# Order of rounding, mask building and copies on VectorE and ScalarE in a two-part transformer kernel: eight small moves between queues

## The chip, the core and the metric

The kernel runs on one core of a Trainium2 chip, batch 1, 256 rows of 1024 features (S = 256, D = 1024). The metric is device time in microseconds (us) of one execution. TensorE (PE) multiplies; VectorE (DVE), ScalarE (ACT) and GpSimd (POOL) do the rest; SyncE (SP) only issues the loads of weights.

## The reference, cut to what matters

```
for i in range(2):                       # first_block
    h = rms_norm(x, norm_mix[i])
    x = x + (dsa_moba_mixer(h, ...) if i == 0 else nsa_mixer(h, ...))
    x = x + memory_cross_attention(rms_norm(x, norm_mem[i]), rms_norm(mem, ...), ...)
    x = x + swiglu(rms_norm(x, norm_ffn[i]), ffn_w_in[i], ffn_w_out[i])
for l in range(2):                       # second_block
    proj = _rmsnorm(x, g_mix[l]) @ w_in[l]
    ...                                  # convolution, neighbourhood, dilated and window attention
    mixed = jnp.sum(gates * branch, axis=2)
    x = x + mixed @ w_out[l]
    x = x + _conv_ffn(_rmsnorm(x, g_ffn[l]), w_up[l], ffn_conv_w[l], ffn_conv_b[l], w_down[l])
```

`rms_norm` divides each row by the root of its mean square. The dilated attention needs a mask that also holds the logarithm of how often a key is counted. Everything is float32.

## The kernel before, in words

Eight blocks of code run one after the other: `block_dsa_moba` (names that begin with ab), `block_memory_ffn` (mf), `block_nsa` (nsa), `block_memory_ffn` again, and then twice `block_branches` (mix) and `block_conv_ffn` (cffn). Each block writes out a queue for each engine by hand; an engine works through its own queue in order, and semaphores are the only ties between queues. The order of the code lines in each queue is therefore the schedule.

**Weights.** Every matrix product is done in three products of rounded parts. A chunk of weights (1 MB, 128x2048) arrives in one of 4 raw slots. ScalarE rounds it (`w.round_to`, L143, writes w_hi), VectorE takes the rest (`w.cut_to`, L144, writes w_lo), and TensorE waits for w_lo. There are 3 slots for the pairs, so rounding chunk c also waits until TensorE has used chunk c - 3. The first four chunks of a block are loaded in the block before, and the first of them is already rounded and cut there. A `stationary_job` is one chunk used as the stationary operand: 48 matmuls of 256 columns. Features are rounded (L297) and cut (L303) in the same way.

**Row factors.** The product is taken before the norm is known. The sums of squares (`rows.square`, L290, ScalarE) go to GpSimd (`rows.factors`, L312 to L318), VectorE spreads the factor (`row_factors.dve`, L332), TensorE turns it (`row_factors.pe`, L338), and ScalarE stores it (`row_factors.act`, L343). In mix and cffn TensorE did this between job 0 and job 1.

**Attention.** `Attention` runs a pipeline over pairs of heads. In step i TensorE makes scores i (L740), turns the exponentials of i - 1 (L750), multiplies with the values of i - 2 (L765) and then does one piece of other work. VectorE masks and takes the maximum (L795), and copies the turned exponentials from PSUM (L810); ScalarE takes the exponential (L778). Scores i wait for the masking of i - 1. In ab VectorE also finds the largest 64 index scores between the steps (`top_rounds`, L1341, L1342), and the other work of TensorE is a third of a memory projection (L882 to L884). In mix it is a whole gate job of 48 matmuls. GpSimd sums the convolution's taps during those steps (L2519).

**Masks.** `make_masks` in mix builds the dilated mask on VectorE in the pauses of the projection: its last piece (j == 2, L2658 to L2668, five operations) stands ahead of the fourth projection's copy (L484). The mask is first used at step 4.

**Tail of mix.** Eight times TensorE forms the four branch products of one tile (L2855 to L2857), VectorE multiplies by the gates (L2771), GpSimd adds (L2528, L2530), ScalarE rounds (L2616) and VectorE cuts (L2758). Cuts of the next chunks stand after every second tile. TensorE may begin tile j only when L2771 of tile j - 2 is done.

## Time and profile before

| | |
|---|---|
| Median of 3 runs | 1686.68 us (1684.48, 1686.98, 1686.68) |
| The profiled execution's own time | 1684.49 us |
| Its span, first to last instruction | 1682.7 us |
| PE busy | 1626.0 us (97%) |
| DVE, ACT, POOL busy | 1096.4, 885.1, 456.2 us |
| Mean granted TensorE clock | 0.995 |

Busy PE time includes the overlap of matmuls in flight, so the pauses between starts of matmuls say more than the share. Line numbers in this part are those of the kernel before.

### The profile page before, as it was taken

Reading aid. Unit: us, or ns where it says so; the run is one execution under the profiler, and the core shown is the slowest. Engines: PE = TensorE matmul, PEld = TensorE weight load, DVE = VectorE, ACT = ScalarE, POOL = GpSimd, SP = SyncE. Lnnn points to the kernel's source line nnn. Section 1 sums busy time; section 2 is a strip of 40 time slices with the busy share of each in tenths; the row PEclk is TensorE's granted clock in tenths of the full one; section 3 lists DMA queues with packets and bytes.
Section 4 is the critical chain, followed back from the end, with each engine's and each line's share of the span. In section 5 each row is a group of like instructions: output and inputs, shape, how many; then the busy total and the mean of one; then the engine's idle time right before and its main releaser. Section 6 shows DMA issues by size and latency. Waiting matters only on the chain. (4 is left out here: it accounts for less than half of the span.)

```text
span 1682.7 us, 26946 instructions
## 1 busy us (share of the span) xinstructions
PE 1626.0 (97%) x10929; PEld 1465.7 (87%) x10929; DVE 1096.4 (65%) x1546; ACT 885.1 (53%) x1385; POOL 456.2 (27%) x476
## 2 busy tenths in 40 slices
PE   8989899999999999999999999999999999999999
PEld 7857799987887879998888998999888899889997
DVE  6875656545576765655577668677646866867773
ACT  7454554434455555443446746566445674665652
POOL 2500200002341120000237805144213790504430
PEclk9999999999999999999999999999999999999999
DMA  7522466556340236665554434766556444376652
GB/s 275 171 75 91 110 181 195 178 199 207 103 150 26 76 101 169 187 193 185 177 191 151 151 126 131 197 182 192 180 160 211 155 150 129 127 197 178 189 187 75
DMA packets 287068, 265.30 MB, mean 158 GB/s; under 512 B 12257, under 2 KB 247521, under 8 KB 286945
## 3 DMA queue, kind: packets, MB, share of 16 engines
q1 hardware_dynamic: 286944, 263.59, 50.4%
q8 instruction: 86, 1.41, 0.4%
q14 instruction: 38, 0.30, 0.1%
HBM read 262.52 MB, written 1.05 MB: 157 GB/s over the span
## 5 line engine op out<-in xcount | busy, mean ns | idle before, releaser
L144 DVE TENSOR_TENSOR w_lo<-w_raw,w_hi 128x2048 fp32r<-128x2048 f32 (+2 forms) x244 | 568.8, 2334 | 296.7 <-ACT w_hi L143 294.5
L1863 PE MATMUL bank<-h_hi,w_hi 128*128 128x256 f32 x1984 | 566.2, 285 | 11.9 <-issue 4.6
L143 ACT ACTIVATE w_hi<-w_raw 128x2048 fp32r<-128x2048 f32 (+2 forms) x244 | 462.4, 1901 | 207.4 <-PE bank L529 117.4
L1864 PE MATMUL bank<-h_lo,w_hi 128*128 128x256 f32 x1984 | 561.9, 283 | 0.0
L1865 PE MATMUL bank<-h_hi,w_lo 128*128 128x256 f32 x1984 | 561.9, 283 | 0.0
L1863 PEld LDWEIGHTS bank<-h_hi,w_hi 128*128 128x128 f32 x1984 | 380.8, 192 | 16.4 <-issue 10.9
L1864 PEld LDWEIGHTS bank<-h_lo,w_hi 128*128 128x128 f32 x1984 | 381.0, 192 | 0.1
L1865 PEld LDWEIGHTS bank<-h_hi,w_lo 128*128 128x128 f32 x1984 | 380.9, 192 | 0.0
L456 PE MATMUL bank<-w_hi,h_hi 128*128 128x512 f32 (+1 forms) x288 | 113.5, 394 | 5.4 <-DVE w_lo L144 3.4
L2925 POOL TENSOR_TENSOR cffn_hidden<-cffn_conv 128x256 f32<-128x256 f32 x44 | 72.2, 1642 | 164.3 <-ACT cffn_conv L2955 164.3
L457 PE MATMUL bank<-w_lo,h_hi 128*128 128x512 f32 (+1 forms) x288 | 111.9, 389 | 0.0
L458 PE MATMUL bank<-w_hi,h_lo 128*128 128x512 f32 (+1 forms) x288 | 111.9, 388 | 0.0
L2519 POOL TENSOR_TENSOR mix_conv<-mix_conv,mix_gates 128x512 f32<-128x512 f32 x60 | 106.2, 1769 | 20.9 <-ACT mix_gates L2556 12.6
L1760 ACT ACTIVATE mf_gate<-mf_gate 128x256 f32<-128x256 f32 x44 | 18.4, 418 | 129.8 <-DVE mf_gate L1809 129.8
L2989 DVE SCALAR_TENSOR_TENSOR cffn_conv<-cffn_before,cffn_cols,cffn_conv 128x255 f32<-128x255 f32 x176 | 75.0, 488 | 0.0
L456 PEld LDWEIGHTS bank<-w_hi,h_hi 128*128 128x128 f32 x288 | 54.3, 189 | 18.8 <-DVE w_lo L144 4.3
L2470 POOL MEMSET mix_padded<- 128x572 f32 x2 | 1.1, 575 | 240.4 <-POOLq L1718 187.2
L458 PEld LDWEIGHTS bank<-w_hi,h_lo 128*128 128x128 f32 x288 | 54.2, 188 | 10.9
L2977 DVE TENSOR_TENSOR cffn_before<-bank,cffn_row_factors 128x512 f32<-128x512 f32 x44 | 30.4, 691 | 50.4 <-PE bank L1865 50.4
L457 PEld LDWEIGHTS bank<-w_lo,h_hi 128*128 128x128 f32 x288 | 54.3, 188 | 10.1
L2556 ACT ACTIVATE mix_gates<-mix_padded,mix_cols 128x256 f32<-128x256 f32 x120 | 50.8, 496 | 14.7 <-POOL mix_conv L2519 14.7
L2528 POOL TENSOR_TENSOR mix_feat<-mix_feat 128x512 f32<-128x512 f32 x16 | 37.7, 2353 | 71.9 <-DVE mix_feat L2771 71.9
(444 smaller groups left out, 2884.0 us busy)
## 6 DMA issues: line engine op xcount, KB each, us to landing
w_raw<-in_w_in SPq DMA_DIRECT2D x48, 1024.0 KB, 5.0
w_raw<-in_ffn_w_in SPq DMA_DIRECT2D x88, 512.0 KB, 5.1
w_raw<-in_w_up SPq DMA_DIRECT2D x88, 512.0 KB, 5.2
w_raw<-in_ffn_w_out SPq DMA_DIRECT2D x22, 1024.0 KB, 4.9
w_raw<-in_w_down SPq DMA_DIRECT2D x22, 1024.0 KB, 4.9
w_raw<-in_nsa_w_in SPq DMA_DIRECT2D x10, 1024.0 KB, 5.1
w_raw<-in_mem_w_kv SPq DMA_DIRECT2D x8, 1024.0 KB, 5.1
w_raw<-in_w_branch SPq DMA_DIRECT2D x8, 1024.0 KB, 5.1
```

What stands on the lines that cost most here:

```text
L143: return act.activation(hi, raw, ACT.Copy)
L144: return dve.tensor_tensor(self.lo[:, cut_slot, 0:k * n], raw, hi.bitcast(F32), ALU.subtract)
L456: pe.matmul(bank, x_hi, whi[:, k, :], start=(f == 0), stop=False)
L457: pe.matmul(bank, x_hi, wlo[:, k, :], start=False, stop=False)
L458: ins = pe.matmul(bank, x_lo, whi[:, k, :], start=False, stop=(f == KD - 1))
L1863: pe.matmul(out, h, hi[:, f, :], start=(f == 0), stop=False)
L1864: pe.matmul(out, h, lo[:, f, :], start=False, stop=False)
L1865: ins = pe.matmul(out, l, hi[:, f, :], start=False, stop=(f == KD - 1))
L2519: pool.tensor_tensor(conv[:, :, :], conv[:, :, :], taps[tap % 4], ALU.add).then_inc(cv_sum, 1)
L2556: act.activation(taps[tap % 4][:, n, :], u, ACT.Copy, scale=weight).then_inc(cv_tap, 1)
L2925: pool.tensor_tensor(hidden[:, j % 2, :], conv[:, j % 2, 0, :], conv[:, j % 2, 1, :], ALU.mult)\
L2989: dve.scalar_tensor_tensor(out=dst, in0=src, scalar=tap(2 * side, tile), in1=dst, op0=ALU.mult, op1=ALU.add).then_inc(sides, 1)
```

## The change

Eight edits to the queues; no arithmetic is added or taken away.

1. In mix and cffn, ScalarE rounds chunk 1 before the squares and chunk 2 behind them, and VectorE cuts chunk 1 before it spreads the factor. TensorE turns the factor in the middle of job 1 instead of between jobs 0 and 1.
2. In ab, the copies of turned exponentials go from VectorE to ScalarE (`copier="act"`), where the copy of pair i - 1 stands behind the exponentials of pair i.
3. In ab, ScalarE rounds the memory chunk before the second memory copy (`act_next(1)` ahead of `act(1)`).
4. In ab, VectorE waits for the turning of the last keys on GpSimd (`hn.wait_done(dve, 5)`) before it cuts the next memory chunk.
5. In ab, the cut of the memory chunk after that goes from before the attention to its step 1.
6. In mix, the five mask operations go to the attention's steps 0 to 3, behind each step's cut.
7. In the tail of mix, one more chunk is cut before tile 0 and none after tile 1.
8. In mf, the first maximum over the scores stands ahead of the second sum of squares.

```diff
@@ Attention.act
+            if i and self.copier == "act":
+                self.copy_turned(act, i - 1)
             if between is not None:
                 between(act, i)
+        if self.copier == "act":
+            self.copy_turned(act, len(self.pairs) - 1)
+
+    def copy_turned(self, e, j):
+        e.wait_ge(self.turned, j + 1)
+        if j >= 2:
+            e.wait_ge(self.out, j - 1)
+        dims = [[S, 2], [1, self.pairs[j]["keys"]]]
+        to, of = free(self.k.turned[:, j % 2, :], dims), free(self.k.bank[6 + j % 2][:, :], dims)
+        if self.copier == "act":
+            e.activation(to, of, ACT.Copy).then_inc(self.copied, 1)
+        else:
+            e.tensor_copy(to, of).then_inc(self.copied, 1)
@@ block_dsa_moba
-        att = Attention(k, "att", pairs, lambda i, u: (4 + u, i % 2 * S))
+        att = Attention(k, "att", pairs, lambda i, u: (4 + u, i % 2 * S), copier="act")
...
                 mem.act(act, 0)
+                mem.act_next(act, 1)
                 mem.act(act, 1)
-                mem.act_next(act, 1)
                 turn.act(act)
...
+                hn.wait_done(dve, 5)
                 mem.dve(dve, 0)
                 dve.wait_ge(const, 2)
-                mem.dve(dve, 1)
                 turn.dve(dve)
...
+                    if i == 1:
+                        mem.dve(dve, 1)
@@ block_memory_ffn
+                att.dve_peaks(dve, 0)
                 att.dve_mean(dve, 1)
-                att.dve_peaks(dve, 0)
@@ stationary_job
+        if tile == 0 and middle is not None:
+            middle(pe)
@@ block_branches, and alike in block_conv_ffn
                 rows.round(act, range(4, KD))
+                w.round_to(act, 1)
                 for t in range(T):
                     rows.square(act, t, 1)
-                w.round_to(act, 1)
+                w.round_to(act, 2)
                 row_factors.act(act)
...
                 rows.cut(dve, range(4, KD))
+                w.cut_to(dve, 1)
                 row_factors.dve(dve)
-                w.cut_to(dve, 1)
...
-                    stationary_job(k, pe, conv_chunks[i], k.bank[6 + i], rows, None, i == 0)
-                    if i == 0:
-                        row_factors.pe(pe)
+                    stationary_job(k, pe, conv_chunks[i], k.bank[6 + i], rows, None, i == 0, row_factors.pe if i else None)
@@ block_branches, masks and tail
+                def behind(dve, i):
+                    cut(dve, AHEAD + i)
+                    make_counts(dve, i)
+
+                att.dve(dve, finish, step, behind)
...
-                w.cut_to(dve, mix_chunks[0] + 1)
+                w.cut_to(dve, mix_chunks[0] + 2)
...
-                    if j % 2 == 1:
+                    if j >= 3 and j % 2 == 1:
                         w.cut_to(dve, mix_chunks[0] + j // 2 + 2)
```

`make_counts` holds the five operations of the old j == 2 piece: two in step 0 and one each in steps 1, 2 and 3.

VectorE's queue at the start of cffn, before (cffn_spread is the spread row factor):

```order
L303 SCALAR_TENSOR_TENSOR h_lo<-bank,ffn_gain,h_hi 128x256 x4
L332 COPY cffn_spread<-row_stat 128x256
L144 TENSOR_TENSOR w_lo<-w_raw,w_hi 128x2048 x2
L2977 TENSOR_TENSOR cffn_before<-bank,cffn_row_factors 128x512
L144 TENSOR_TENSOR w_lo<-w_raw,w_hi 128x2048
```

The same place of the changed kernel (L2977 is now L2999):

```order
L303 SCALAR_TENSOR_TENSOR h_lo<-bank,ffn_gain,h_hi 128x256 x4
L144 TENSOR_TENSOR w_lo<-w_raw,w_hi 128x2048
L332 COPY cffn_spread<-row_stat 128x256
L144 TENSOR_TENSOR w_lo<-w_raw,w_hi 128x2048
L2999 TENSOR_TENSOR cffn_before<-bank,cffn_row_factors 128x512
```

One cut went ahead of the spread; the other stayed between the spread and the first scaled product.

ScalarE's queue in ab from the memory copies (mem_kv) into the attention, before (ab_att is the buffer of the exponentials):

```order
L901 ACTIVATE mem_kv<-bank,ab_mem_stat 128x512 x2
L143 ACTIVATE w_hi<-w_raw 128x2048
L404 ACTIVATE ab_feat<-bank 128x512 x6
L404 ACTIVATE ab_feat<-bank 128x256
L778 ACT_TABLE_LOAD
L778 ACTIVATE ab_att,ab_att_stat<-ab_att,ab_att_stat 128x128 x8
L778 ACTIVATE ab_att,ab_att_stat<-ab_att,ab_att_stat 128x256 x8
```

The same place of the changed kernel, up to the fourth pair (L901 is now L909, and L797 is the copy):

```order
L909 ACTIVATE mem_kv<-bank,ab_mem_stat 128x512
L143 ACTIVATE w_hi<-w_raw 128x2048
L909 ACTIVATE mem_kv<-bank,ab_mem_stat 128x512
L404 ACTIVATE ab_feat<-bank 128x512 x6
L404 ACTIVATE ab_feat<-bank 128x256
L778 ACT_TABLE_LOAD
L778 ACTIVATE ab_att,ab_att_stat<-ab_att,ab_att_stat 128x128 x4
L797 ACTIVATE ab_att<-bank 128x2x128
L778 ACTIVATE ab_att,ab_att_stat<-ab_att,ab_att_stat 128x128 x2
L797 ACTIVATE ab_att<-bank 128x2x128
L778 ACTIVATE ab_att,ab_att_stat<-ab_att,ab_att_stat 128x128 x2
```

The rounding went between the two memory copies, and a copy stands behind each pair's exponentials from the second pair on.

VectorE's queue in mix around the masks, before (mix_centred and mix_sig serve as scratch):

```order
L661 TENSOR_TENSOR mix_proj<-mix_proj,mix_vectors 128x2x256
L2658 TENSOR_SCALAR mix_centred<-mix_dil 128x512
L2660 TENSOR_SCALAR mix_sig<-mix_dil 128x512
L2663 TENSOR_TENSOR mix_centred<-mix_centred,mix_sig 128x512
L2665 TENSOR_SCALAR mix_sig<-mix_dil 128x512
L2668 TENSOR_TENSOR mix_dil<-mix_centred,mix_sig 128x512
L484 TENSOR_SCALAR mix_proj<-bank,row_stat 128x512
```

In the changed kernel they stand in the attention; of its steps 1 and 2 (L811 masks, L2725 is a gate's product, L799 the copy):

```order
L144 TENSOR_TENSOR w_lo<-w_raw,w_hi 128x2048
L2674 TENSOR_SCALAR mix_centred<-mix_dil 128x512
L2675 TENSOR_SCALAR mix_sig<-mix_dil 128x512
L811 ISA mix_att,mix_att_stat<-bank,mix_bias 128x256
L811 ISA mix_att_stat 128x1
L811 ISA mix_att,mix_att_stat<-bank,mix_bias 128x256
L811 ISA mix_att_stat 128x1
L2725 TENSOR_TENSOR mix_gates<-bank,mix_row_factors 128x512
L799 COPY mix_att<-bank 128x512
L144 TENSOR_TENSOR w_lo<-w_raw,w_hi 128x2048
L2679 TENSOR_TENSOR mix_centred<-mix_centred,mix_sig 128x512
```

The fourth projection's copy now follows the head norm at once, and the masking of steps 1 to 4 has mask work ahead of it.

## Rows read from the trace of the kernel before

**Rows 1.** The page: span, and busy time of the engines.

```profile
span 1682.7 us, 26946 instructions
PE 1626.0 (97%) x10929; PEld 1465.7 (87%) x10929; DVE 1096.4 (65%) x1546; ACT 885.1 (53%) x1385; POOL 456.2 (27%) x476
```

**Rows 2.** What PE waited for: us in total, times, longest us.

```profile
PE bank L1863 <- issue: 4.6, 4, 2.1
PE bank L2855 <- DVE mix_feat L2771: 4.1, 4, 1.3
PE bank L1527 <- ACT mf_att L1600: 3.9, 2, 2.0
PE bank L1863 <- DVE w_lo L144: 3.8, 4, 1.2
PE bank L765 <- DVE ab_att L810: 3.8, 4, 1.4
```

**Rows 3.** Timeline, start of the first mix block: start, duration, instruction, idle before.

```profile
827.69 1.57 ACT L297 ACTIVATE h_hi<-bank,mix_gain 128x256 fp32r<-128x256 f32 x4 [2.97 <-PEq L1718]
...
832.91 2.27 DVE L144 TENSOR_TENSOR w_lo<-w_raw,w_hi 128x2048 fp32r<-128x2048 f32 x1
...
833.62 0.38 PE L338 MATMUL bank<-ident,mix_att 128*128 128x128 f32 x2
835.23 0.39 PE L1863 MATMUL bank<-h_hi,w_hi 128*128 128x256 f32 x1 [1.23 <-DVE w_lo L144]
```

**Rows 4.** Timeline of PE, start of the second cffn block.

```profile
1497.45 0.38 PE L338 MATMUL bank<-ident,cffn_spread 128*128 128x128 f32 x2
1498.51 0.39 PE L1863 MATMUL bank<-h_hi,w_hi 128*128 128x256 f32 x1 [0.68 <-DVE w_lo L144]
```

**Rows 5.** Timeline, end of the memory projection in ab.

```profile
84.93 1.91 ACT L143 ACTIVATE w_hi<-w_raw 128x2048 fp32r<-128x2048 f32 x1
86.73 3.29 ACT L404 ACTIVATE ab_feat<-bank 128x512 f32<-128x512 f32 x7
...
90.08 0.49 PE L740 MATMUL bank<-ab_feat 64*128 64x128 f32 x4 [1.30 <-ACT ab_feat L404]
```

**Rows 6.** Timeline, attention steps 4, 9 and 11 in ab.

```profile
97.22 0.70 PE L740 MATMUL bank<-ab_feat 64*128 64x256 f32 x4
...
115.32 2.29 DVE L144 TENSOR_TENSOR w_lo<-w_raw,w_hi 128x2048 fp32r<-128x2048 f32 x1
...
119.90 0.80 PE L740 MATMUL bank<-ab_feat 64*128 64x128 f32 x4
```

**Rows 7.** Stretch; length, busy PE, PEld, DVE, ACT, POOL (x), PEclk, DMA share, GB/s.

```profile
118.60:125.40 6.80, 6.80 (x26) 4.43 (x25) 4.84 (x20) 1.62 (x9) 0.00 (x0) 0.50 0.47 154
```

**Rows 8.** Timeline, end of the projection in the first mix block.

```profile
884.83 0.69 ACT L470 ACTIVATE mix_proj<-bank,row_stat 128x512 f32<-128x512 f32 x1 [4.46 <-PE bank L458]
...
887.21 0.74 DVE L484 TENSOR_SCALAR mix_proj<-bank,row_stat 128x512 f32<-128x512 f32 x1
...
888.11 1.65 POOL L674 TENSOR_TENSOR mix_hn_stat<-mix_hn_stat,half_power 128x8 f32<-128x8 f32 x1
...
891.59 2.30 DVE L144 TENSOR_TENSOR w_lo<-w_raw,w_hi 128x2048 fp32r<-128x2048 f32 x1
```

**Rows 9.** Timeline of POOL, convolution sums of the first mix block.

```profile
899.22 4.12 POOL L2519 TENSOR_TENSOR mix_conv<-mix_conv,mix_gates 128x512 f32<-128x512 f32 x3
909.63 25.45 POOL L2519 TENSOR_TENSOR mix_conv<-mix_conv,mix_gates 128x512 f32<-128x512 f32 x13 [6.29 <-ACT mix_gates L2556]
```

**Rows 10.** Timeline, tail of the first mix block.

```profile
1012.04 1.91 ACT L143 ACTIVATE w_hi<-w_raw 128x2048 fp32r<-128x2048 f32 x1
...
1018.75 2.28 DVE L144 TENSOR_TENSOR w_lo<-w_raw,w_hi 128x2048 fp32r<-128x2048 f32 x1
...
1024.27 1.29 DVE L2771 TENSOR_TENSOR mix_feat<-bank,mix_gates 128x512 f32<-128x512 f32 x2
```

**Rows 11.** Timeline of DVE, memory attention of the first mf block.

```profile
180.16 0.69 DVE L1637 TENSOR_REDUCE mf_q_stat<-mf_q_squared 128x4 f32<-128x512 f32 x1 [1.69 <-ACT mf_q_squared L1579]
```

More of the change, by code:

```diff
@@ L701, with __init__ @@
 class Attention:
-    def __init__(self, k, name, pairs, place=None):
+    def __init__(self, k, name, pairs, place=None, copier="dve"):
         s = k.sems
-        self.k, self.pairs = k, pairs
+        self.k, self.pairs, self.copier = k, pairs, copier
         self.place = place or (lambda i, u: (4 + i % 2, u * S))
@@ L801, in dve @@
                 between(dve, i)
-            if 1 <= i <= n:
-                j = i - 1
-                p = self.pairs[j]
-                dve.wait_ge(self.turned, j + 1)
-                if j >= 2:
-                    dve.wait_ge(self.out, j - 1)
-                w = p["keys"]
-                dims = [[S, 2], [1, w]]
-                dve.tensor_copy(free(self.k.turned[:, j % 2, :], dims), free(self.k.bank[6 + j % 2][:, :], dims))\
-                    .then_inc(self.copied, 1)
+            if 1 <= i <= n and self.copier == "dve":
+                self.copy_turned(dve, i - 1)
             if i >= 3 and self.pairs[i - 3]["last"]:
@@ L1847, in block_memory_ffn, with stationary_job @@
         k.close()
-def stationary_job(k, pe, c, bank, features, free_bank, first=False):
+def stationary_job(k, pe, c, bank, features, free_bank, first=False, middle=None):
     w, hi, lo = k.weights, features.hi, features.lo
@@ L2654, in make_masks, with make_counts @@
                                     .then_inc(mask_step, 1)
-                    if j == 2:
-                        count, value = centred[:, :, :], sig[:, :, :]
+                def make_counts(dve, i):
+                    count, value = centred[:, :, :], sig[:, :, :]
+                    if i == 0:
                         dve.wait_ge(mask_step, 7)
                         dve.tensor_scalar(count, dil[:, :, :], 0.0, NEG, ALU.is_equal, ALU.mult).then_inc(mask_step, 1)
-                        dve.wait_ge(cv_mul, 2)
                         dve.tensor_scalar(value, dil[:, :, :], 2.0, 8 * math.log(2.0), ALU.is_equal, ALU.mult)\
                             .then_inc(mask_step, 1)
+                    if i == 1:
                         dve.wait_ge(mask_step, 9)
                         dve.tensor_tensor(count, count, value, ALU.add).then_inc(mask_step, 1)
+                    if i == 2:
                         dve.wait_ge(mask_step, 10)
@@ L2666, in make_masks @@
                             .then_inc(mask_step, 1)
+                    if i == 3:
                         dve.wait_ge(mask_step, 11)
                         dve.tensor_tensor(dil[:, :, :], count, value, ALU.add).then_inc(mask_step, 1)
+                        dve.wait_ge(mask_step, 12)
                 def bias_table(dve):
@@ L2690, in sums @@
                         w.cut_to(dve, project.last[j] + 3)
-                    if j < 3:
+                    if j < 2:
                         make_masks(dve, j)
@@ L2745, in _ @@
                 dve.wait_ge(biased, 1)
-                dve.wait_ge(mask_step, 12)
-                att.dve(dve, finish, step, lambda dve, i: cut(dve, AHEAD + i))
+                def behind(dve, i):
+                    cut(dve, AHEAD + i)
+                    make_counts(dve, i)
+                att.dve(dve, finish, step, behind)
                 dve.wait_ge(ln_act, 3)
@@ L2935, in _ @@
                 rows.round(act, range(4, KD))
+                w.round_to(act, 1)
                 for t in range(T):
                     rows.square(act, t, 1)
-                w.round_to(act, 1)
+                w.round_to(act, 2)
                 row_factors.act(act)
@@ L2965, in _ @@
                 rows.cut(dve, range(4, KD))
+                w.cut_to(dve, 1)
                 row_factors.dve(dve)
-                w.cut_to(dve, 1)
                 dve.wait_ge(cols_in, 16)
@@ L2999, in _ @@
                 for j in range(KF):
-                    stationary_job(k, pe, up[j], k.bank[j % 4], rows, (scaled, j - 3) if j >= 4 else None, j == 0)
-                    if j == 0:
-                        row_factors.pe(pe)
+                    stationary_job(k, pe, up[j], k.bank[j % 4], rows, (scaled, j - 3) if j >= 4 else None, j == 0,
+                                   row_factors.pe if j == 1 else None)
                 down.pe(pe, lambda pe, f: pe.wait_ge(hid_lo, f + 1))
```

## The prediction, made before the changed kernel ran

> **What bounds the kernel.** I read the page first. TensorE is busy for 1626.0 us of a span of 1682.7 [rows 1], so at most 56.7 us of visible pauses can be won, whatever the other engines do. The next view is the list of what TensorE waited for; a handful of waits carry most of it, and the change touches five of them [rows 2]: 3.8 us in four waits of a stationary job for a cut (w_lo), 4.6 us in four waits put down to "issue", 3.8 us in four waits of the value products for VectorE's copies in ab, 4.1 us in four waits in the tail of mix, 3.9 us in two waits for the first exponentials in mf. Together that is 20.2 us. The timeline around each then tells what ended last, and what would end last next. The profiled execution took 1684.49 us, 1.8 more than its span; the other two runs took about 2.3 us more than it.
>
> **Term 1, row factors.** In the first mix block TensorE turned the factors from 833.62, which takes 0.23 us, and job 1 began at 835.23 [rows 3]: 1.38 us lost to the cut of chunk 1, which began at 832.91 because the squares and the factor stood ahead. Now ScalarE starts rounding when the features are done at 829.26 [rows 3] and takes 1.9 us [rows 5], and VectorE cuts from 831.15 to 833.4 (2.27). That is just in time for job 0's end at 833.62. The squares slip by 1.9 us and the factor is spread at about 834.1; TensorE wants it in the middle of job 1, which is 24 matmuls or 2.9 us behind 833.6, so at 836.5. That leaves 2.4 us. Chunk 2 is cut by about 837.5 (two rounds of 1.9 and a cut), and wanted when job 1 ends at 839.6. So the stall goes and I see none in its place. In cffn the same arithmetic gives 1498.51 - 1497.45 - 0.23 = 0.83 [rows 4], and the cut of chunk 1 is over at about 1497.3 against a job that ends at 1497.45. Two mix and two cffn blocks: 2 x 1.38 + 2 x 0.83 = **4.4 us**. Lower bound 2.5, if the cut of chunk 1 comes half a microsecond late four times; upper 4.4.
>
> **Term 2, attention in ab.** First the moved rounding: ScalarE rounded at 84.93 for 1.9 us and only then copied the seven turned groups, and the first scores waited for the last copy until 90.08 [rows 5]. The rounding now fits into the wait between the two memory copies, so the copies start near 84.9 and end near 88.2: 1.8 us won. The new wait of VectorE for GpSimd costs nothing: nothing else is queued behind it but a cut that TensorE wants near 88.7, and it lets GpSimd finish before that cut. The cut moved into step 1 does cost. It is 2.29 us [rows 6] ahead of the masking of step 2, VectorE has some 0.9 us of slack there, and scores 3 wait for that masking: 1.4 us lost. So step 4 begins only 0.4 us sooner than 97.22 [rows 6].
>
> From there VectorE does not copy any more, and the four waits for its copies, 3.8 us [rows 2], go. In their place: behind the exponentials of step 7 ScalarE now has a copy (0.6), the memory copy (0.6) and a rounding (1.9), 3.1 us ahead of the exponentials of step 8, of which TensorE's step hides 2.0; 1.1 us lost. In step 9 the cut of 2.29 us still delays the masking of step 10, 0.5 us lost. Sum: 1.8 - 1.4 + 3.8 - 1.1 - 0.5 = **2.6 us**.
>
> The clock comes on top. TensorE was granted half its clock (1.2 instead of 2.4 GHz) from 118.6 to 125.4 [rows 7], directly behind two of these waits, and was busy throughout: at full clock the same work takes 3.4 us less, or 2.9 if the waits that would show again are taken off. With the waits gone I expect the fall not to come, **2.9 us**; the bounds are 0 and 3.4. Step 11 would then begin near 115.8 instead of 119.90 [rows 6].
>
> **Term 3, masks.** VectorE's copy of the fourth projection began at 887.21 though ScalarE's began at 884.83 [rows 8]: the five mask operations were in between, 2.4 us. What follows, however, waits for GpSimd as well: its power for the third head norm ended at 889.76 [rows 8], and only then comes the norm and the cut of the second gate chunk at 891.59, for which TensorE waited (two of the waits called "issue", up to 2.1 us [rows 2]). If GpSimd gains nothing, the head norm starts 0.4 us sooner; if GpSimd runs unhindered while VectorE is idle, it ends near 889.0 and the cut starts 1.3 us sooner. I take 1.2: the mask operations ran beside GpSimd's, and they are the only work there that leaves. Two blocks: **2.4 us**, between 0.8 and 4.2.
>
> In the attention of mix the same 2.8 us of VectorE lie in four steps of 7 us or more, each with some 3 us of idle VectorE. The masking of a step comes 0.4 to 1.0 us later, the copy too, and TensorE wants that copy at the earliest 2 us after it is ready now. Cost zero while that cover holds; if it is gone, each step costs what is above it.
>
> Here a rule speaks against the change. A sum of GpSimd takes 4.12/3 = 1.37 us while VectorE is quiet and 25.45/13 = 1.96 us in the attention [rows 9], so the two do hinder each other. The Trainium skill, SBUF — State Buffer, "Who interferes with whom", has it that VectorE with two SBUF inputs, or in a two-port mode, and GpSimd share a port pair, and whoever is first blocks the other for the whole instruction. By that rule each of the five mask operations could wait for one sum of 1.96 us [rows 9], 9.8 us per block on top of their own 2.8; by the overlap seen in the rows they cost their own 2.8.
>
> **Term 4, tail of mix.** Tile 3's product began at 1024.27, of which 2.28 us was the cut at 1018.75 [rows 10]. The cut now waits for its rounding, 1012.04 + 1.91 = 1013.95 [rows 10], ends at 1016.3, and holds back tile 0's product by 1.6 us, which costs TensorE 0.3 at tile 2. After that VectorE waits for TensorE, not the other way: tile 3 is multiplied at 1023.5 instead of 1024.27. From there on the rhythm of 7.3 us per two tiles is VectorE's in both kernels. So of 2.28 us 0.75 stays: **1.5 us** for two blocks, between -0.6 (only the 0.3) and 1.8.
>
> **Term 5, the maximum.** The sum of squares at 180.16 takes 0.69 and waits for ScalarE [rows 11]; the scores were ready about 1 us before. The exponentials then come 1.1 us sooner, and 3.9 us of waits [rows 2] shrink to 1.8. But the next product waits for a copy behind a cut and for GpSimd's factor, both of which move by 0.3 at most. **0.4 us** for both, between -0.8 (GpSimd's factor falls behind the cut) and 1.5.
>
> **Sum.** 4.4 + 2.6 + 2.9 + 2.4 + 1.5 + 0.4 = 14.2 us, so 1684.5 - 14.2 = 1670.3 against the profiled execution. The median of before lies 2.2 above that execution; I take 0.7 of it, since part of it may be the same falls of the clock: **1671 us**.
>
> **Rivals.** (a) The stalls in ab return elsewhere and the clock falls all the same. For it: ScalarE's 3.1 us behind step 7, and the moved cut; against: each of the new waits, 1.1 and 1.4 us, is at most as long as the longest that goes, 1.4 [rows 2]. Term 2 and the clock then give 0 instead of 5.5, and term 3 its lower 0.8: 14.2 - 5.5 - 1.6 = 7.1, or 1684.5 - 7.1 = about 1677.5. (b) The change does not do what it says: the cut of chunk 1 ends after job 0 and GpSimd holds the norm, so only scraps of each wait go. Then about 2 us are won, 1683. (c) Slower: mask operations wait for GpSimd's sums, the masking and the copy come late, and TensorE waits in steps 1 to 4 of mix. The price is 12.6 us per block by the rule's count, minus the cover of about 2 us in each of four steps, so 4.6 per block or 9 in both; that alone gives 1679.5. It turns the sign only if the cover is gone altogether: 2 x 12.6 = 25 against 14.2, or 1684.5 + 11 = 1695. It decides from 2.2 us of wait per step on. Against it: VectorE is idle in each step.
>
> **Chances.** A difference of less than 0.2% (3.4 us) is what a measurement of this kernel can hardly tell from none. Forecast with its own range 1666 to 1676: 0.62. (a) and the mild form of (c), 1676 to 1681: 0.24. (b): 0.08. (c) in full: 0.06. The range 1664 to 1681 leaves out (b), (c) in full and a bit below, in which nearly all falls of the clock would vanish. Faster 0.87, same 0.08, slower 0.05.
>
> **What the new profile would show.** Right: no wait of L1873 for w_lo at the start of mix and cffn; the first scores in ab near 88.3, scores 11 near 116; one wait of L750 or L765 near step 9 on ScalarE; the second gate job of mix 1 us sooner after the turned groups; the wait behind tile 5 in the tail near 1.0; clock 1.0 throughout ab. Wrong: waits for masking or copies in the first four steps of mix, a half clock in ab, or a head norm that still starts 5 us after the projection's end.

## The result, and the profile after

The changed kernel took 1664.05 us (median of 4 runs, 1663.56 to 1664.86) beside 1685.71 us for the kernel before (4 runs, 1684.48 to 1686.98): a ratio of 0.9872, with a 95% interval of 0.9855 to 0.9889. The forecast was 1671 us with a range of 1664 to 1681. The sign and the places were right, and the size was too small by a third: 21.7 us came where some 15 had been expected, so that the time lies on the range's lower edge: two of the four executions fall inside the range and two below it. That it was met is luck. Line numbers from here on are those of the changed kernel, unless a row is said to be of before.

The page of the changed kernel, beside [rows 1]:

```profile
span 1661.8 us, 26943 instructions
PE 1618.9 (97%) x10929; PEld 1461.4 (88%) x10929; DVE 1097.6 (66%) x1530; ACT 891.5 (54%) x1401; POOL 450.3 (27%) x476
```

The span is 20.9 us shorter with the same 10929 matmuls, and TensorE's busy time fell by 7.1 us as well. Less busy time for the same work can't be a wait that went: it is the clock, and the first hint that two things happened. The list of TensorE's waits (us in total, times, longest), beside [rows 2]:

```profile
PE bank L1537 <- ACT mf_att L1610: 1.8, 2, 0.9
PE bank L750 <- ACT ab_att L778: 1.5, 3, 0.9
PE bank L2876 <- DVE mix_feat L2794: 1.5, 2, 0.7
PE bank L1546 <- DVE mf_att L1680: 1.3, 2, 0.6
PE bank L1873 <- issue: 1.2, 4, 0.4
```

L1873 does not wait for w_lo any more and L765 not for a copy; "issue" fell from 4.6 to 1.2, the tail from 4.1 to 1.5, the exponentials of mf from 3.9 to 1.8. One wait is new, 0.8 us of L740 in ab, and two are longer: L1546 in mf and L750 in ab, which before stood at 0.3 and 0.4 us (below).

To see where the time came from I laid the starts of the same matmuls of both traces side by side and noted where the distance between them jumps. What a stretch at half clock cost is read in the same way, as the time that the same matmuls take more than in the trace that has the full clock there. The 6.8 us of [rows 7] cost 3.1, not 3.4: their matmuls take about 1.8 times as long as at full clock, not twice (118.00 to 125.58 in the trace of before, 114.11 to 118.57 in the changed kernel's). A stretch of 3.4 us costs 1.5 to 1.6.

| Part | Forecast | Measured |
|---|---|---|
| 1, row factors, two mix and two cffn | 4.4 | 4.9 (1.50 and 0.93 each) |
| 2, waits in ab | 2.6 | 3.8 |
| 2, half clock in ab | 2.9 | 3.1 |
| 3, masks, two mix | 2.4 | 3.4 (1.7 each) |
| 4, tail, two mix | 1.5 | 2.4 (1.2 each) |
| 5, maximum, two mf | 0.4 | 1.2 (0.6 each) |
| half clock in mf and nsa | none | 2.1 |
| sum | 14.2 | 20.9 |

### The profile page after: what moved, and what is told of

Read it like the earlier page. It is cut to its first block and busy times, and to the rows that moved or that the text cites. A ratio compares the mean times of both kernels' runs of the same rounds, so it can differ in the third digit from the quotient of the medians.

```text
span 1661.8 us, 26943 instructions
## 1 busy us (share of the span) xinstructions
PE 1618.9 (97%) x10929; PEld 1461.4 (88%) x10929; DVE 1097.6 (66%) x1530; ACT 891.5 (54%) x1401; POOL 450.3 (27%) x476
## 5 line engine op out<-in xcount | busy, mean ns | idle before, releaser
L1873 PE MATMUL bank<-h_hi,w_hi 128*128 128x256 f32 x1984 | 565.5, 285 | 4.7 <-issue 1.2
L1873 PEld LDWEIGHTS bank<-h_hi,w_hi 128*128 128x128 f32 x1984 | 380.5, 192 | 8.2 <-issue 7.5
L2999 DVE TENSOR_TENSOR cffn_before<-bank,cffn_row_factors 128x512 f32<-128x512 f32 x44 | 30.4, 691 | 49.4 <-PE bank L1875 48.7
L778 ACT ACTIVATE mix_att<-mix_att,mix_att_stat 128x256 f32<-128x256 f32 x48 | 24.0, 501 | 61.5 <-PE bank L750 39.6
L526 PE MATMUL bank<-w_lo,mf_wide_hi 128*128 128x512 f32 x144 | 56.0, 389 | 0.0
```

The lines of the kernel that those rows point to most:

```text
L526: pe.matmul(self.bank[2 * t + half][:, :], x_hi, wlo[:, k, columns], start=False, stop=False)
L1873: pe.matmul(out, h, hi[:, f, :], start=(f == 0), stop=False)
```

## The rows behind the table

**The first mix block** (timeline of the changed kernel, ScalarE, VectorE and TensorE) went as forecast: the rounding stands ahead of the squares, the cut of chunk 1 is over at 823.10, just 0.2 us before job 1 begins at 823.33, the factor is spread later, and the factors are turned inside job 1.

```profile
818.85 1.93 ACT L143 ACTIVATE w_hi<-w_raw 128x2048 fp32r<-128x2048 f32 x1
...
820.81 2.29 DVE L144 TENSOR_TENSOR w_lo<-w_raw,w_hi 128x2048 fp32r<-128x2048 f32 x1 [0.87 <-ACT w_hi L143]
824.25 1.14 DVE L332 COPY mix_att<-row_stat 128x256 f32<-128x256 f32 x1 [1.15 <-POOL row_stat L318]
...
826.21 0.38 PE L338 MATMUL bank<-ident,mix_att 128*128 128x128 f32 x2
```

**ab.** The first scores start at 88.27 (forecast 88.3), scores 11 at 115.36 (forecast 115.8, before 119.90 [rows 6]). The rows show the two prices that I had set against the gain: the cut in step 1 with 0.79 us of idle TensorE behind it, and ScalarE's row of copy, memory copy and rounding behind step 7 with 0.86.

```profile
88.27 0.49 PE L740 MATMUL bank<-ab_feat 64*128 64x128 f32 x4 [1.14 <-ACT ab_feat L404]
...
91.56 2.29 DVE L144 TENSOR_TENSOR w_lo<-w_raw,w_hi 128x2048 fp32r<-128x2048 f32 x1
...
94.33 0.49 PE L740 MATMUL bank<-ab_feat 64*128 64x128 f32 x4 [0.79 <-DVE ab_att_stat L811]
...
107.37 0.57 ACT L797 ACTIVATE ab_att<-bank 128x512 f32<-128x512 f32 x1
107.85 0.67 ACT L909 ACTIVATE mem_kv<-bank,ab_mem_stat 128x512 f32<-128x512 f32 x1
108.42 1.90 ACT L143 ACTIVATE w_hi<-w_raw 128x2048 fp32r<-128x2048 f32 x1
110.22 0.39 ACT L778 ACTIVATE ab_att<-ab_att,ab_att_stat 128x128 f32<-128x128 f32 x1
...
111.14 0.44 PE L750 MATMUL bank<-ident,ab_att 128*128 128x128 f32 x2 [0.86 <-ACT ab_att L778]
```

**End of the projection in mix.** What was [rows 8] now reads as below. VectorE copies at the same moment as ScalarE, and GpSimd's six rotations take 0.32 us each, 872.87 to 874.72. Before, the five that ran beside the mask operations took 0.44 to 0.77 each and the last one 0.32, together 3.1 us from the first's start to the last's end (six rows from 884.65 on in the trace of before). So the power ends 3.68 us behind the start of ScalarE's copy instead of 4.93.

```profile
872.87 0.32 POOL L692 TENSOR_TENSOR mix_rope_parts<-mix_proj,rope_tables 128x64 f32<-128x64 f32 x1 [4.36 <-DVE mix_proj L661]
...
873.05 0.75 DVE L484 TENSOR_SCALAR mix_proj<-bank,row_stat 128x512 f32<-128x512 f32 x1 [0.27 <-PE bank L458]
...
875.08 1.65 POOL L674 TENSOR_TENSOR mix_hn_stat<-mix_hn_stat,half_power 128x8 f32<-128x8 f32 x1
...
876.76 0.69 DVE L656 TENSOR_TENSOR mix_proj<-mix_proj,mix_hn_stat 128x512 f32<-128x512 f32 x1 [0.56 <-POOL mix_hn_stat L674]
...
878.10 2.30 DVE L144 TENSOR_TENSOR w_lo<-w_raw,w_hi 128x2048 fp32r<-128x2048 f32 x1
```

**The mask operations in the attention of mix.** They cost TensorE nothing, but they did get long: 8.1 us per block instead of 2.8. Three of the five groups of VectorE in the first mix block (busy us, mean ns of one):

```profile
L2679 DVE TENSOR_TENSOR mix_centred<-mix_centred,mix_sig 128x512 f32<-128x512 f32 x1 | 1.8, 1784 | 0.0
L2686 DVE TENSOR_TENSOR mix_dil<-mix_centred,mix_sig 128x512 f32<-128x512 f32 x1 | 1.8, 1777 | 0.0
L2674 DVE TENSOR_SCALAR mix_centred<-mix_dil 128x512 f32<-128x512 f32 x1 | 1.5, 1522 | 0.0
```

**The clock.** Stretches of before (length, busy PE, PEld, DVE, ACT, POOL, and then the granted clock): besides [rows 7] three more at half clock, one in mf and two in nsa (the third, at 432.6, isn't shown).

```profile
183.50:186.90 3.40, 3.40 (x11) 2.84 (x11) 2.51 (x4) 1.36 (x5) 1.24 (x1) 0.50 0.24 67
480.40:483.80 3.40, 3.40 (x9) 2.63 (x8) 3.33 (x9) 0.98 (x1) 3.12 (x10) 0.50 0.00 0
```

Of the changed kernel, the work of mf and the one stretch at half clock that is left, in nsa:

```profile
174.90:181.70 6.80, 6.16 (x43) 5.18 (x44) 6.19 (x11) 4.95 (x14) 2.52 (x3) 1.00 0.50 139
470.20:473.50 3.30, 3.10 (x7) 2.48 (x8) 3.27 (x10) 1.51 (x2) 2.94 (x9) 0.50 0.05 19
```

## The experiments

All start from the changed kernel. Each ran on one chip with runs of the kernel before beside it; times are medians of 4 to 6 runs. Since a median moves by 1 us or more for reasons that have nothing to do with an edit (last section), what an edit cost is read in the trace: how much later than in the changed kernel a matmul behind the edit's place starts, minus the same for one ahead of it.

### 1. Copies on VectorE again

```
-        att = Attention(k, "att", pairs, lambda i, u: (4 + u, i % 2 * S), copier="act")
+        att = Attention(k, "att", pairs, lambda i, u: (4 + u, i % 2 * S))
```

> The changed kernel, with the turned attention values of ab copied by VectorE again; everything else stays. My theory: each wait has its own cause and the terms add. The waits of the value products (3.8 us in four waits before) come back, the wait of 1.03 us behind step 7 on ScalarE goes. The attention of ab ends 2.8 us later, 1664.05 + 2.8 = about 1667, and up to 3.4 more if the half clock near its end comes back with the waits. Rival 1: the moved rounding made the gain, VectorE has slack enough to copy: less than 0.8 us. Rival 2: the half clock has nothing to do with these waits: the waits come back, 2.8 us, and the clock stays whole.

1674.38 us (1669.4 to 1675.14), 10.3 more than the changed kernel, and 10.4 in the trace from the start to the end of ab. No theory had that. The first value product has a wait that neither kernel had: its copy stands behind the cut in step 1.

```profile
91.62 2.29 DVE L144 TENSOR_TENSOR w_lo<-w_raw,w_hi 128x2048 fp32r<-128x2048 f32 x1
93.83 0.42 DVE L799 COPY ab_att<-bank 128x256 f32<-128x256 f32 x1
```

```profile
PE bank L765 <- DVE ab_att L799: 5.7, 5, 1.9
```

Five waits, 5.7 us, instead of four and 3.8 [rows 2]. And two stretches at half clock, each of 6.8 us and each directly behind one of these waits (of 2.0 us at 92.2, of 1.6 at 119.7, measured from start to start). The first of them:

```profile
94.40:101.10 6.70, 6.70 (x24) 4.60 (x24) 2.74 (x16) 1.76 (x8) 0.00 (x0) 0.50 0.46 157
```

By the starts of the same matmuls each of the two costs 3.1 us, 6.2 of the 10.4; the other 4.2 are waits. This is one execution. The six have mean clocks of 0.993 to 0.997, and the one of 0.997 took 1669.4 us, so not each has both stretches. The edits of ab don't add: the cut can stand in step 1 only because ScalarE copies.

### 2. The cut ahead of the attention again

```
                 mem.dve(dve, 0)
                 dve.wait_ge(const, 2)
+                mem.dve(dve, 1)
...
-                    if i == 1:
-                        mem.dve(dve, 1)
```

> The changed kernel, with VectorE's cut of the second memory chunk in ab ahead of the attention again, not in step 1. Theory: the cut, 2.29 us, then lies from 87.45 to 89.74 and the first masking comes 0.8 us later than its 88.95; in return the two waits of 0.96 and 0.43 us in step 1 and 2 go. Net 0.6 us won, about 1663.5. Rival: the cut also holds back VectorE's part of the turned groups or GpSimd, and the first scores come 1 us or more later; then it is level or up to 1.5 us slower, 1664 to 1665.5.

1665.1 us (1663.74 to 1667.66). In the trace the first masking is at 89.74 to the hundredth, the waits of 0.96 and 0.43 us are gone, and then the clock fell behind two waits of 1.3 and 0.65 us, in a stretch in which the changed kernel keeps its full clock:

```profile
90.60:93.90 3.30, 3.22 (x15) 1.95 (x13) 1.66 (x11) 1.49 (x7) 0.00 (x0) 0.50 1.02 408
```

Over the whole of ab the kernel lost 0.35 us: what the queue gives, the clock takes, and a little more. Another 1.6 us went in nsa, which the edit does not touch. Its four runs have mean clocks of 0.998, 0.997, 0.995 and 0.998. So most of the 1.4 us that my forecast charged for the moved cut is there (1.2 us against the same matmuls of before), but leaving the cut where it was would not have saved them.

### 3. No wait for GpSimd ahead of the first cut in ab

```
-                hn.wait_done(dve, 5)
```

> The changed kernel, without VectorE's wait for GpSimd's last rotation ahead of the cut in ab. Theory: the cut starts near 82.4 beside GpSimd's rotations, one of them takes 2.45 us as before instead of 0.46, the last head norm and with it the first scores come later than 88.27: by 0.8 to 2 us, about 1665.4. Rival: ScalarE's rounding until 84.3 sets the first scores anyhow: no change.

1665.84 us (1665.5 to 1666.21). In the trace the first scores are 0.8 us later and the end of ab 1.1, the first theory's lower half. GpSimd's first rotation (L692) stands beside the cut and takes 2.44 us, the five others 0.46 each:

```profile
83.33 2.44 POOL L692 TENSOR_TENSOR ab_rope_parts<-ab_proj,rope_tables 128x128 f32<-128x128 f32 x1 [3.37 <-DVE ab_proj L661]
```

The added wait is worth about 1 us. I had priced it at nothing and put the whole 1.8 us down to the moved rounding; they are worth that only together.

### 4. Mask operations behind the fourth copy

```
                 project.dve(dve, sums, hurry=3)
+                for i in range(4):
+                    make_counts(dve, i)
...
-                    make_counts(dve, i)
```

> The changed kernel, with the five mask operations of mix in the projection again, but behind VectorE's copy of the fourth projection instead of ahead of it. Two readings of why 1.7 us per block were won where 1.2 was forecast. (1) GpSimd now runs its rotations and its power (1.65 us) without VectorE beside it: with the operations behind the copy the power ends later, the cut starts 0.5 to 2 us later than 878.10, and the wait of 0.58 us ahead of the second gate job grows to 1.1 to 2.6: 1 to 4 us for both blocks, 1665 to 1668. (2) Only the late copy counted: it stays early, and the time stays 1664.0.

1673.13 us (1671.34 to 1673.59), 9.1 more: outside both readings. The timeline shows why this was a poor test of them. Everything up to the head norm is as in the changed kernel, with rotations of 0.32 us and a power of 1.65 us; the five operations then lie between the head norm and the cut for which TensorE waits, and their 2.7 us go straight onto its path.

```profile
879.34 0.44 DVE L2674 TENSOR_SCALAR mix_centred<-mix_dil 128x512 f32<-128x512 f32 x1
...
882.06 2.29 DVE L144 TENSOR_TENSOR w_lo<-w_raw,w_hi 128x2048 fp32r<-128x2048 f32 x1
```

TensorE stops for 3.28 us instead of 0.58, and at 884.7, behind that wait, its clock halves, in both mix blocks:

```profile
884.70:888.00 3.30, 3.30 (x17) 3.30 (x17) 3.30 (x3) 0.00 (x0) 3.30 (x2) 0.50 0.74 242
```

2.7 us of wait and 1.5 of clock per block make the 8.4 us that the two blocks lost in the trace. That GpSimd's rotations were slowed by the mask operations before rests on the rows of the two kernels alone, not on this run.

### 5. All mask operations in one step

```
-                    make_counts(dve, i)
+                    if i == 0:
+                        for n in range(4):
+                            make_counts(dve, n)
```

> The changed kernel, with all five mask operations in step 0 of mix's attention instead of one or two in each of four steps. In four steps they took 8.1 us per block and cost TensorE nothing. If the length of 1.5 to 1.8 us each (0.4 to 0.7 alone) is a wait for GpSimd's running sum, the five take 7 to 9 us in a row here, VectorE has 3 to 4 us of idle time in a step, so the next masking is some 4 us late and TensorE, with about 2 us of cover, waits 1.5 to 3 us per block: 1667 to 1670. If operations in a row keep GpSimd out after the first, they take 4 to 5 us and cost 0 to 0.5 per block: 1664 to 1665.

1673.85 us (1673.69 to 1675.14), 9.8 more. This is rival (c) brought about. VectorE and GpSimd in step 0 of the first mix block:

```profile
898.21 1.52 DVE L2674 TENSOR_SCALAR mix_centred<-mix_dil 128x512 f32<-128x512 f32 x1
...
901.21 1.67 DVE L2679 TENSOR_TENSOR mix_centred<-mix_centred,mix_sig 128x512 f32<-128x512 f32 x1
902.91 1.37 DVE L2682 TENSOR_SCALAR mix_sig<-mix_dil 128x512 f32<-128x512 f32 x1
904.31 0.69 DVE L2686 TENSOR_TENSOR mix_dil<-mix_centred,mix_sig 128x512 f32<-128x512 f32 x1
```

```profile
896.84 7.15 POOL L2531 TENSOR_TENSOR mix_conv<-mix_conv,mix_gates 128x512 f32<-128x512 f32 x4 [6.30 <-ACT mix_gates L2569]
```

GpSimd's four sums end at 903.99. The addition that starts behind them takes 0.69 us, as when VectorE is alone; the same addition at 901.21, beside them, takes 1.67. So the length is GpSimd's doing, operation by operation. The sums taken one by one end at 899.45, 900.89, 902.33 and 904.00, the four long operations at 899.73, 901.17, 902.88 and 904.28: each ends 0.3 to 0.6 us behind the end of a sum. The Trainium skill (SBUF — State Buffer, "Who interferes with whom") says that of VectorE, with two SBUF inputs or in a two-port mode, and GpSimd, whoever is first blocks the other for the whole instruction. The trace agrees with that: an operation loses what is left of the running sum, about 1 us, not the 1.96 of a whole sum that I had put into the rival. In a row they took 6.8 us, and TensorE waited twice, for 3.2 us each:

```profile
PE bank L740 <- DVE mix_att_stat L811: 6.4, 2, 3.2
```

6.8 us late, 3.4 us of wait from start to start: TensorE has some 3.4 us of cover in this step, not 2. With the clock that is 4.95 us per block. In the changed kernel the two operations of step 0 delay it by 2.9 us (897.51 to 900.39), and the other steps hold one operation each. The margin is narrow, and once it was gone the clock fell here too, at 908.0 and 1334.6.

### 6. Row factors as before

```
-                w.round_to(act, 1)
                 for t in range(T):
                     rows.square(act, t, 1)
-                w.round_to(act, 2)
+                w.round_to(act, 1)
...
-                w.cut_to(dve, 1)
                 row_factors.dve(dve)
+                w.cut_to(dve, 1)
...
-                    stationary_job(k, pe, conv_chunks[i], k.bank[6 + i], rows, None, i == 0, row_factors.pe if i else None)
+                    stationary_job(k, pe, conv_chunks[i], k.bank[6 + i], rows, None, i == 0)
+                    if i == 0:
+                        row_factors.pe(pe)
```

These are the lines of mix; in cffn the same was done.

> The changed kernel, with the row factors of both mix and both cffn blocks as before: one chunk rounded, behind the squares, the factors turned between job 0 and job 1. Theory: the wait ahead of job 1 comes back with 1.5 us per mix and 0.9 per cffn block, 4.8 us: 1668.9. Rival: part of what was read there went to pauses elsewhere or to the phase of the clock: 2 to 3 us only, or more than 6.

1669.69 us (1668.61 to 1670.07), 5.6 more. The waits are back as they were in [rows 2]:

```profile
PE bank L1873 <- DVE w_lo L144: 3.8, 4, 1.2
```

The four places lose 1.50, 0.92, 1.51 and 0.93 us in the trace, 4.9 us in all, to the tenth what the comparison of the two kernels gave. No stretch at half clock came with them in mix or cffn, though two waits of 1.5 us did. In the same trace another 0.7 us went in nsa and 0.9 at the program's start (last section), where nothing was changed.

### 7. The tail's third chunk cut behind tile 1 again

```
-                w.cut_to(dve, mix_chunks[0] + 2)
+                w.cut_to(dve, mix_chunks[0] + 1)
...
-                    if j >= 3 and j % 2 == 1:
+                    if j % 2 == 1:
```

> The changed kernel, with the cut of the tail's third chunk behind tile 1 again in both mix blocks. Theory: tile 3's product again stands behind that cut, the wait of 0.9 becomes 2.35 us: 1.2 per block, 1666.4. Rival, my forecast's own arithmetic: 0.75 per block, 1665.5.

1666.48 us (1665.94 to 1666.7), 2.4 more, as the first theory had it, and 2.4 in the trace: in each block 0.3 us are won at tile 2, 0.9 lost at tile 4 and 0.6 at tile 6, and nothing anywhere else. My 0.75 held only part of it. VectorE's product of tile 3, the cut behind it and the product of tile 4, in this run:

```profile
1010.84 1.29 DVE L2794 TENSOR_TENSOR mix_feat<-bank,mix_gates 128x512 f32<-128x512 f32 x2
1012.04 2.83 DVE L144 TENSOR_TENSOR w_lo<-w_raw,w_hi 128x2048 fp32r<-128x2048 f32 x1
1016.40 1.29 DVE L2794 TENSOR_TENSOR mix_feat<-bank,mix_gates 128x512 f32<-128x512 f32 x2
```

and in the changed kernel:

```profile
1010.15 1.29 DVE L2794 TENSOR_TENSOR mix_feat<-bank,mix_gates 128x512 f32<-128x512 f32 x2 [0.71 <-PE bank L2878]
1011.35 2.28 DVE L144 TENSOR_TENSOR w_lo<-w_raw,w_hi 128x2048 fp32r<-128x2048 f32 x1
1015.16 1.29 DVE L2794 TENSOR_TENSOR mix_feat<-bank,mix_gates 128x512 f32<-128x512 f32 x2
```

Tile 3 is 0.7 us sooner, as forecast, but the cut behind it is also 0.55 us shorter, 2.28 instead of 2.83 us. The rhythm of 7.3 us per two tiles, which I took to be VectorE's own, held that longer cut. In the rows the long cuts start beside an addition of GpSimd (L2542, 0.74 us long, from 1011.99 in this run), while the short one of the changed kernel starts when that addition is all but over (it ends at 1011.42). No run separates the two.

### 8. The maxima of mf in the old order

```
-                att.dve_peaks(dve, 0)
                 att.dve_mean(dve, 1)
+                att.dve_peaks(dve, 0)
```

> The changed kernel, with the second sum of squares ahead of the first maximum in both mf blocks again. Theory: the wait for the first exponentials is 2.1 instead of 1.08 us and the wait of 0.90 behind the cut goes in part, 0.6 us per block, so +1.2. For the clock two theories: if the half clock of 183.5 to 186.9 (before) followed from this order of waits, it comes back and costs 1.5 us more in a block: up to 1668. If it came from what the program did in all the time before it, it stays away and the kernel takes 1665.3.

1667.1 us (1665.75 to 1668.31). The wait for the first exponentials is 2.12 us again, from start to start, and the one ahead of L1546 is 0.35 instead of 0.90. The blocks lose 0.65 and 0.58 us, the forecast 1.2 in all; another 0.85 us is the program's start (last section). Of the two theories on the clock the second held in the profiled execution. The very wait behind which the clock fell before is back, and it did not fall:

```profile
176.80:183.60 6.80, 6.70 (x47) 5.63 (x48) 6.18 (x11) 5.41 (x14) 1.82 (x1) 1.00 0.55 153
```

Two of the four executions took 2.4 us more than this one, 1668.3 us, with the same mean clock to three digits. They have no trace, and one stretch of 3.4 us at half clock more would move that mean by only 0.001, so a fall in them isn't ruled out.

### 9. The wait that is new in mf, attacked in two ways

VectorE copies the first turned group of mf behind a cut and a maximum, at 177.91, and TensorE waits 0.90 us for it. First the cut was put off:

```
-                w.cut_to(dve, residual.first + 1)
                 att.dve_peaks(dve, 2)
...
                 att.dve_out(dve, 0)
+                w.cut_to(dve, residual.first + 1)
                 att.dve_store(dve, 1)
```

> The changed kernel, with VectorE's cut of the second residual chunk in both mf blocks moved from between the maxima to behind the first half's output. Theory: the wait of 0.90 us ahead of the value product (177.62) is that cut's, and goes; GpSimd's stretched operation (1.60 us beside the cut) gets short too. 0.9 per block: 1662.2. Rival: the transfer into that chunk's buffer starts 10 us later and TensorE waits for it at the start of the next part, or the cut (184.3 to 186.6) holds back the second half's output, wanted at 187.2: then as long as now or longer, up to 1666.

1665.66 us (1665.05 to 1665.71). The wait shrinks to 0.36 us, but 0.68 us come instead, since TensorE wants that chunk only 1.5 us behind the first matmul of the residual, and the second half's output is late as well. Each block lost 0.4 us, as in the rival:

```profile
187.07 0.50 PE L546 MATMUL bank<-w_hi,h_hi 128*128 128x512 f32 x1 [0.52 <-DVE w_lo L144]
```

Then the copy was given to ScalarE, which sits idle there (`act_turned_first` waits for the turned group 0 and copies it from its bank):

```
                 att.act_exps(act, 1)
+                att.act_turned_first(act)
                 att.act_exps(act, 2)
...
-                att.dve_turned(dve, 0)
```

> The changed kernel, with the first turned group of both mf blocks copied by ScalarE behind its second pair of exponentials, not by VectorE behind the cut and a maximum. Theory: the wait of 0.90 us ahead of the value product (177.62) ends when VectorE's copy of 177.91 is done; ScalarE sits idle from 176.4 to 178.1, so the copy comes 1.4 us sooner and the wait goes: 0.9 per block, 1662.3. Rival: the next exponentials or the copy of the second group wait for it instead and TensorE stops one step later, as when the cut was moved: 1664 to 1665.

1664.28 us (1662.95 to 1664.75). Here the rival was half right. The copy is at 176.24 and the wait is gone, but 0.45 us of idle TensorE come one step later, behind exponentials whose maximum still stands behind the cut. The net is 0.3 us won in each block, too little for the median.

```profile
176.24 0.61 ACT L1678 ACTIVATE mf_att<-bank 128x512 f32<-128x512 f32 x1
...
178.03 0.56 ACT L1610 ACTIVATE mf_att<-bank,mf_att_peak,mf_q_stat 128x256 f32<-128x256 f32 x1 [1.18 <-DVE mf_att_peak L1673]
...
179.28 0.66 PE L1537 MATMUL bank<-ident,mf_att 128*128 128x128 f32 x4 [0.45 <-ACT mf_att L1610]
```

### 10. ScalarE's rounding in ab behind step 11

```
-                    if i == 7:
+                    if i == 11:
                         mem.act_next(act, 2)
...
-                    if i == 9:
+                    if i == 13:
                         mem.dve(dve, 2)
```

> The changed kernel, with ScalarE's rounding behind step 7 of ab's attention moved behind step 11 and VectorE's cut of it from step 9 to step 13. Theory: behind step 7 it stood with a copy and the memory copy, 3.1 us in a row, for a wait of 1.03 us; behind step 11 ScalarE has 1.18 us idle, so exponentials 12 come 0.7 us late, of which TensorE's step hides part: 0.5 us won, 1663.5. Rival: the cut in step 13, 2.3 us, delays the maskings of the longer steps behind it and costs as much again, or the weights' next transfer is late at the block's end: 1664.5 to 1666.

1663.87 us (1663.28 to 1663.91). The wait of 1.03 us behind step 7 went, one of 0.54 came at 118.8, and ab is 0.64 us shorter (its last turning starts at 130.90 instead of 131.48). The cut in step 13 cost nothing.

### 11. Both additions

> The changed kernel with both additions: the first turned group of mf copied by ScalarE, and the rounding of ab behind step 11. The traces of the two alone show 0.4 to 0.5 us less per mf block and 0.5 us less in ab. If they add, as the sites lie apart, 1.4 us less than the changed kernel: 1662.6. Rival: at this size the clock and the start of the first transfers decide, and it measures the same as the changed kernel, 1663.5 to 1665.

1663.55 us (1662.42 to 1664.66; ratio to before 0.9874, interval 0.9858 to 0.9891). The two add: ab wins 0.67 us and the mf blocks 0.30 and 0.35, 1.3 in all. In the same trace 0.8 us went at the program's start, and 1.6 us went in nsa, where the stretch at half clock lies elsewhere (478.5 instead of 470.1). So the time is not to be told from the changed kernel's. The rival held: 1.3 us are won in the queues, and no version here measurably beats the changed kernel.

## Why the prediction was right in kind and too small

**What bounds the kernel.** Right: of five waits named, each shrank or went, and at its own place.

**Term 1, row factors,** 4.4 forecast, 4.9 measured, 4.9 when undone. The difference is some 0.1 us behind each wait, which shows from start to start and not in the idle time that I added up.

**Term 2, ab.** The first scores and step 4 came at their hour, 88.3 and 96.7. Step 11 came at 115.4 where 115.8 was forecast, but that is luck: the terms of the forecast make 2.6 us by then, and the 1.3 us of half clock ahead of 119.90 some 0.65, so they give 116.6. Two sizes were off. The waits for VectorE's copies are 4.5 us from start to start (0.8, 0.6, 1.5, 1.6), not the 3.8 of the list, and the cut in step 9, charged with 0.5 us, cost nothing. The moved cut cost 1.2, not 1.4. Against that stands a wait of 0.4 us at 101.6 that I had not counted, 0.2 longer than the one before. And of the 1.8 us at the start nearly half hangs on the added wait for GpSimd (experiment 3), which I had put at zero.

**The clock in ab.** The half clock went, and it was worth 3.1 us where I had 2.9. My reasons for both figures were off: the work at half clock was not 3.4 us of work at full clock but 3.7, and the waits that I took off don't show at full clock. Experiment 1 shows the link in one direction. With the copies back on VectorE the waits come back, and in its trace the half clock with them, at the same wait as in before and at one more.

**Term 3, masks,** 2.4 forecast, 3.4 measured: the step that failed is the 889.0 that I gave for the end of GpSimd's power when unhindered. By the rows after it is 1.25 us sooner than 889.76, that is 888.5, and then it is GpSimd and not VectorE that the head norm waits for. In the attention the operations were hidden, as forecast, by a cover that in step 0 is about 3.4 us rather than 2; the other steps' was not measured.

**Term 4, tail,** 1.5 forecast, 2.4 measured: "the rhythm of 7.3 us per two tiles is VectorE's in both kernels" was the wrong step. It held a cut stretched to 2.83 us, which takes 2.28 when it starts 0.7 us sooner (experiment 7). What stretches it was not tried; its neighbour on GpSimd is the suspect.

**Term 5, the maximum,** 0.4 forecast, 1.2 measured. The first wait went from 2.12 to 1.08 us as forecast; behind it came 0.90 where 0.35 had been, so with small waits less elsewhere about 0.45 us of each 1.04 were given back, and I had allowed for nearly all of it.

**What I left out** are 2.1 us of half clock in mf and nsa, places that the change hardly touches. Together with the terms (0.5, 1.4, 1.0, 0.9 and 0.8) that is the missing 6.7 us. The prediction itself had named this case, "a bit below, in which nearly all falls of the clock would vanish", and left it outside the range. Why they went is not settled. For mf, experiment 8 speaks against the obvious cause, the order of the maxima: with the old wait back the clock stayed whole in the trace. In nsa a stretch near 423 comes and goes between kernels that are identical there. The second version of experiment 9 has it at 422.1, with the same matmuls only 0.3 us earlier than in the changed kernel, which does not have it. So the waits and their order alone do not settle whether the clock falls.

**The rivals.** (a), new waits and a clock that falls again, did not come about, but is real: experiment 2 is such a case. (b) did not come about. (c) had its mechanism right, and experiment 5 its price: 9.9 us in the trace as soon as the operations stand in one step, where it had allowed 25 at most.

## What to carry to other kernels

In this kernel, where TensorE runs at 97%, a wait could cost twice: once itself and, in some places and executions, once more as a stretch at half clock behind it. Price such a change with the clock's share in the range, at both ends, for every stretch of half clock in the trace and not only for the one at the edit. Second, the list of waits counts idle time only; sums by the distance of the matmuls' starts were 0.1 to 0.2 us per wait larger, and nearer to what was won. Third, work moved into idle time of VectorE has its length there only if GpSimd is quiet: read its duration from a row with the same neighbour, and spread it over several steps: four steps hid here what cost 9.9 us in one with some 3.4 us of cover.

## What was not expected of the hardware

**The kernel before is unsteady, and the changed one was not in its four runs.** The 35 runs of before that stood beside the experiments have spans from 1678.7 us, at a mean granted clock of 0.998, to 1687.8 us at 0.992, and in between the two mostly go together: 1680.5 to 1682.4 at 0.997, 1682.5 to 1683.0 at 0.995, 1683.3 to 1685.0 at 0.994. They do not always: of six at 0.996 three span 1681.7 to 1681.9 and three 1684.4 to 1684.6, and two at 0.993 only 1684.2 and 1684.4. One stretch of 3.4 us at half clock is 0.001 of the mean and 1.5 to 1.6 us of time. The four runs of the changed kernel span 1661.8 to 1663.1 us at 0.998 and 0.999. At 0.998 the two are about 16 us apart (1678.7 and 1678.9 beside 1662.1 to 1663.1); that is the change's share of waits, and the table has 15.7. The rest of the 21.7 us is then clock.

**When the clock fell.** All stretches at half clock in ab, mf and mix began within 2.5 us behind the end of a wait of 1.3 to 3.4 us (from start to start) and were 3.4 or 6.8 us long; but waits of 2.1 (experiment 8), 1.45 (experiment 7) and 1.5 us (experiment 6) went by without one. A wait of 3.3 us had one in all four cases (experiments 4 and 5, two blocks each).

**A start that varies.** In every trace TensorE begins to turn the first rows of the input at 5.8 to 6.0 us. What varies is the clock. The traces hold no granted clock for the first microseconds, and the first one on record, full clock, starts at 5.9 us in the changed kernel's, at 7.5 to 8.3 in those of experiments 3, 4, 6, 8, 11 and the first half of 9, and at 6.8 in experiment 5's. Until it does, the same sixteen matmuls take longer; here are the changed kernel and experiment 8:

```profile
5.84 1.99 PE L279 MATMUL bank<-ident,x_rows 128*128 128x128 f32 x16
```

```profile
5.85 2.95 PE L279 MATMUL bank<-ident,x_rows 128*128 128x128 f32 x16
```

All that follows is 0.8 to 1.0 us later in these traces, and 0.4 in experiment 5's. A median that differs by 1 us says nothing of an edit here; the trace at the edit's place does.
